# A gated convolution's input product in quarters: seven products of quarters in place of eight

## The reference, cut to what matters

```python
def shortconv(z, w):
    zp = jnp.pad(z, ((0, 0), (1, 1), (0, 0)))
    return w[0] * zp[:, :-2] + w[1] * zp[:, 1:-1] + w[2] * zp[:, 2:]

def odd_mixer(h, w_in, conv_w, w_out):
    bg, cg, u = jnp.split(h @ w_in, 3, axis=-1)
    return (bg * shortconv(cg * u, conv_w)) @ w_out
```

## Time and profile before

| what | value |
|---|---|
| median of three runs | 2458.86 us (2455.47 to 2461.43) |
| span of the profiled execution, first to last instruction | 2454.7 us |
| TensorE busy | 2323.3 us (95%) |
| VectorE busy | 855.8 us (35%) |
| input product of the gated convolution | 1705.74 to 1872.10 us of the span |

### The profile page before, as it was taken

The page is one execution under the profiler, slowest core; times in us unless marked ns, Lnnn a source line. Parts: engine busy times, 40 slices in busy tenths (PEclk is TensorE's granted clock), DMA queues, the critical chain, the costliest instruction groups (busy, mean ns, idle before and its releaser), DMA issues.

```text
span 2454.7 us, 22347 instructions
## 1 busy us (share of the span) xinstructions
PE 2323.3 (95%) x8986; PEld 1089.8 (44%) x8986; DVE 855.8 (35%) x1230; ACT 367.1 (15%) x697; POOL 65.3 (3%) x70
## 2 busy tenths in 40 slices
PE   7999899999999999879799999998999799999997
PEld 3443344444444455555544444443444454444443
DVE  3882354467006650782302222113111312222223
ACT  3224200001004110461210000002000110000000
POOL 1000000000010000000000000000000100000000
PEclk9999999999999999999899999999999799999999
DMA  9227234668300102000499999998010479999995
GB/s 356 111 73 274 86 137 157 234 236 328 142 0 26 43 35 69 35 1 1 206 412 421 429 428 428 429 427 307 11 57 1 205 312 429 429 428 429 429 428 229
DMA packets 105646, 565.62 MB, mean 230 GB/s; under 512 B 8424, under 2 KB 17006, under 8 KB 77934
## 3 DMA queue, kind: packets, MB, share of 16 engines
q1 hardware_dynamic: 104880, 563.55, 56.7%
q10 hardware_dynamic: 702, 1.18, 0.1%
HBM read 562.61 MB, written 2.10 MB: 230 GB/s over the span
## 4 chain that ended last, share of the span: by engine, by line
PE 83%; DMA 10%; DVE 5%; ACT 1%; issue 1%; SPq 0%; DVEq 0%; ACTq 0%
PE psum L973 38%; PE psum L1425 19%; DMA ring<-in_moe_w_gate_dram 7%; PE psum L1484 5%; PE psum L1440 5%; PE psum L1242 3%; PE psum L1353 2%; PE psum L1115 1%; DMA ring<-in_moe_w_down_dram 1%; DMA ring<-in_conv_w_pw_dram 1%; PE psum L1317 1%; PE psum L993 1%; DVE small L1766 1%; PE psum L1290 1%; PE psum L1033 1%
## 5 line engine op out<-in xcount | busy, mean ns | idle before, releaser
L1425 PE MATMUL psum<-ring,arena 128*64 128x512 f32 x3072 | 671.5, 595 | 20.3 <-DMA ring<-in_moe_w_gate_dram 13.0
L973 PE MATMUL psum<-hT,ring 128*128 128x512 f32 x1504 | 657.8, 598 | 15.0 <-ACT hT L665 12.0
L973 PEld LDWEIGHTS psum<-hT,ring 128*128 128x128 f32 x1504 | 287.4, 192 | 378.1 <-issue 366.1
L1425 PEld LDWEIGHTS psum<-ring,arena 128*64 128x64 f32 x3072 | 228.4, 137 | 449.0 <-issue 446.9
L973 PE MATMUL psum<-arena,ring 128*128 128x512 f32 x640 | 278.1, 593 | 0.0
L973 PEld LDWEIGHTS psum<-arena,ring 128*128 128x128 f32 x640 | 120.5, 190 | 149.7 <-issue 149.5
L1906 DVE TENSOR_TENSOR hT<-hT,psum 128x512 f32<-128x512 f32 x128 | 88.0, 687 | 244.1 <-PE psum L1484 244.1
L1440 PE MATMUL psum<-arena 128*128 128x128 f32 x1024 | 124.3, 281 | 4.0 <-DVE arena L1915 4.0
L1440 PEld LDWEIGHTS psum<-arena 128*128 128x128 f32 x1024 | 120.1, 197 | 15.5 <-issue 15.5
L1484 PE MATMUL psum<-arena 128*128 128x512 f32 x256 | 123.2, 619 | 0.0
L1578 DVE SCALAR_TENSOR_TENSOR xT<-psum,modv,xT 128x512 f32<-128x512 f32 x32 | 24.0, 751 | 246.0 <-PE psum L973 202.8
(11 more groups left out here) (216 smaller groups left out, 1636.2 us busy)
## 6 DMA issues: line engine op xcount, KB each, us to landing
ring<-in_moe_w_gate_dram SPq DMA_DIRECT2D x64, 2048.0 KB, 14.8
ring<-in_moe_w_up_dram SPq DMA_DIRECT2D x64, 2048.0 KB, 16.4
ring<-in_moe_w_down_dram SPq DMA_DIRECT2D x64, 2048.0 KB, 16.8
ring<-in_ada_w_dram SPq DMA_DIRECT2D x24, 2048.0 KB, 12.9
ring<-in_mlp_w_dram SPq DMA_DIRECT2D x16, 2048.0 KB, 11.4
ring<-in_w_mod_dram SPq DMA_DIRECT2D x12, 2048.0 KB, 12.8
ring<-in_conv_w_in_dram SPq DMA_DIRECT2D x6, 2048.0 KB, 18.7
ring<-in_attn_w_in_dram SPq DMA_DIRECT2D x5, 2048.0 KB, 8.0
```

The lines of the kernel that those rows point to most:

```text
L973: ins = pe.matmul(bank[:, 0:width], w[:, k, col:col + P], src(k), start=start and k == 0, stop=stop and k == kts - 1)
L1425: ins = pe.matmul(psum[64 * e:64 * e + 64, bank + nh, :], src[:, 4 * h + k, 64 * e:64 * e + 64], w[:, k, nh * N:(nh + 1) * N], start=h == ...
```

## The change

Each block of 1024x512 weights (a "unit", six of them in `UNITS`) is cut into four quarters of 512 rows by 256 columns, and `hT` into four quarters of 512 features by 256 tokens. The four quarters of the result come from seven products of quarters rather than eight, with the sums of Strassen's scheme in Winograd's form. Each product is 8 matmuls of 128x128 weights by 256 tokens: four for each half of a PSUM bank.

- VectorE forms three new sums of weights in SBUF and one in place for each unit (`w_sums`), and once four sums of the activations (`h_sums`), one of them in place.
- TensorE makes the products in a hand-written order in four banks for each unit; in three of them a second product is added onto the first.
- ScalarE copies the first product (M1) to SBUF, as TensorE then adds onto the same bank; for part 1 it also copies one finished quarter.
- VectorE adds the products up (`unit_out`) and multiplies each part into the one before it; `shortconv` runs the taps over four pieces at once in the program's order.
- The slots are released at the end of each unit. The memset of `hT` on GpSimd waits for the last tile of the last unit, and the output product waits for `mixed` by halves of four pieces.

```diff
-    for half in range(2):
-        for j in range(4 * half, 4 * half + 4):
-            T_O[j] = tiles(["act", "dve", "dve"])
...
+    for part, half in UNITS:
+        T_U.append(tiles(["dve", "act" if part == 1 else "dve", "dve", "dve"]))
+        add(blk(A["conv_w_in_2"][0], 0, part * D + half * N), ("tile_done", T_U[-1] + 4))
...
+            for u, (part, half) in enumerate(UNITS):
+                t = T_U[u]
+                act.wait_ge(S["part_done"], 3 * u + 1)
+                if u:
+                    act.wait_ge(*emptied(T_U[u - 1])(0))
+                act.activation(m1_sb, bank_pair(t + 1), ACT.Copy).then_inc(S["m1_copied"], 1)
+                if part == 1:
+                    act.wait_ge(S["tile_done"], t + 2)
...
+            def product(t, w, src, first=False):
+
+                for i in range(2):
+                    for k in range(4):
+                        ins = pe.matmul(psum[:, t % 6, H * i:H * i + H], w[:, k, P * i:P * i + P], src[:, k, :],
+                                        start=first and i == 0 and k == 0, stop=True, skip_group_check=True)
+                return ins
+
+            for u in range(len(UNITS)):
+                t = T_U[u]
+                slot = stream[oo + u][1]
+                arrived(pe, oo + u)
+                begin(t + 1)
+                if u == 0:
+                    pe.wait_ge(S["h_ready"], 8 * BIASED[MIX1] + 4)
+                product(t + 1, w_quarter(slot, 0, 0), hT[:, 0:4, 0:H], True).then_inc(S["part_done"], 1)
+                begin(t + 3)
+                if u == 0:
+                    pe.wait_ge(S["hsum_ready"], 1)
+                pe.wait_ge(S["wsum_ready"], 4 * u + 1)
+                product(t + 3, wsum[3 * u % 4], hsum1, True).then_inc(S["part_done"], 1)
+                begin(t)
+                if u == 0:
+                    pe.wait_ge(S["hsum_ready"], 2)
+                pe.wait_ge(S["wsum_ready"], 4 * u + 3)
+                product(t, wsum[(3 * u + 1) % 4], hsum2, True).then_inc(S["tile_done"], 1)
+                begin(t + 2)
+                if u == 0:
+                    pe.wait_ge(S["hsum_ready"], 4)
+                product(t + 2, w_quarter(slot, 0, 1), hsum3, True).then_inc(S["part_done"], 1)
+                pe.wait_ge(S["m1_copied"], u + 1)
+                product(t + 1, w_quarter(slot, 1, 0), hT[:, 4:8, 0:H]).then_inc(S["tile_done"], 1)
+                pe.wait_ge(S["part_read"], 2 * u + 1)
+                product(t + 2, w_quarter(slot, 1, 1), hsum4).then_inc(S["tile_done"], 1)
+                pe.wait_ge(S["wsum_ready"], 4 * u + 4)
+                pe.wait_ge(S["part_read"], 2 * u + 2)
+                product(t + 3, wsum[(3 * u + 2) % 4], hT[:, 4:8, H:N]).then_inc(S["tile_done"], 1)
...
+            def w_sums(u):
+
+                slot = stream[FIRST + u][1]
+                arrived(dve, FIRST + u)
+                s1, s2, s4 = (wsum[(3 * u + m) % 4] for m in range(3))
+                a11, a12, a21, a22 = (w_quarter(slot, r, c) for r, c in ((0, 0), (1, 0), (0, 1), (1, 1)))
+                dve.tensor_tensor(s1, a21, a22, ALU.add).then_inc(S["wsum_ready"], 1)
+                dve.tensor_tensor(a21, a11, a21, ALU.subtract).then_inc(S["wsum_ready"], 1)
+                dve.wait_ge(S["wsum_ready"], 4 * u + 1)
+                dve.tensor_tensor(s2, s1, a11, ALU.subtract).then_inc(S["wsum_ready"], 1)
+                dve.wait_ge(S["wsum_ready"], 4 * u + 3)
+                dve.tensor_tensor(s4, a12, s2, ALU.subtract).then_inc(S["wsum_ready"], 1)
+
+            def h_sums():
+
+                b11, b21 = hT[:, 0:4, 0:H], hT[:, 4:8, 0:H]
+                b12, b22 = hT[:, 0:4, H:N], hT[:, 4:8, H:N]
+                dve.wait_ge(S["h_ready"], 8 * BIASED[MIX1] + 4)
+                dve.tensor_tensor(hsum1, b12, b11, ALU.subtract).then_inc(S["hsum_ready"], 1)
...
+            def unit_out(u):
...
+                dve.wait_ge(S["tile_done"], t + 1)
+                dve.wait_ge(S["m1_copied"], u + 1)
+                dve.tensor_tensor(u2_sb, m1_sb, bank_pair(t), ALU.add).then_inc(FREE["dve"], 1)
+                dve.wait_ge(FREE["dve"], tile_free[t][1])
+                dve.wait_ge(S["part_done"], 3 * u + 3)
+                dve.tensor_tensor(u3_sb, u2_sb, bank_pair(t + 2), ALU.add).then_inc(S["part_read"], 1)
+                dve.wait_ge(S["part_read"], 2 * u + 1)
+                z22 = z[:, 2:4, H:N]
+                dve.tensor_tensor(z22 if part == 1 else u3_sb, u3_sb, bank_pair(t + 3), ALU.add)\
+                    .then_inc(S["part_read"], 1)
+                dve.wait_ge(S["part_read"], 2 * u + 2)
+                if part != 1:
+                    link(fold(z22, u3_sb))
+                if u + 1 < len(UNITS):
+                    w_sums(u + 1)
...
+            link(dve.memset(zpad[:, :, 0:1], 0.0))
+            link(dve.memset(zpad[:, :, N + 1:N + 2], 0.0))
+            w_sums(0)
             scale(MIX1, xT, hT, gain[:, 5, :])
...
+            h_sums()
+            for u in range(len(UNITS)):
+                unit_out(u)
```

More of the change, by code:

```diff
@@ L201, in block_kernel @@
     assert FIRST % RING == 0
-    T_O = {}
-    order_o = []
+    T_U = []
+    UNITS = [(part, half) for half in range(2) for part in (1, 2, 0)]
     T_H, T_AFF, T_POS = {}, {}, {}
@@ L359, in block_kernel @@
         prob1 = carve(arena, 8192, NK)
[L361 to L364, removed]
+        zpad = carve(arena, 0, 4, N + 2)
+        mixed = carve(arena, 4 * (N + 2), DT, N)
+        m1_sb, u2_sb, u3_sb = (carve(arena, 6152 + N * m, 2, H) for m in range(3))
+        wsum = [carve(arena, 8192 + 1024 * m, 4, H) for m in range(4)]
+        hsum1, hsum2 = (x[:, :, :].rearrange("p a b -> p (a b)").rearrange("p (k n) -> p k n", k=4) for x in (sq, tmp))
+        hsum4 = carve(K, KCOL["cos"][0], 4, H)
+        hsum3 = hT[:, 0:4, H:N]
         h_tok = carve(arena, 0, NT, D)
@@ L615, in _ @@
                 sum_squares(ROUTED[layer])
-                pool.wait_ge(S["tile_done"], T_WO + 8 if layer == 0 else T_O[DT - 1] + 3)
+                pool.wait_ge(S["tile_done"], T_WO + 8 if layer == 0 else T_U[-1] + 4)
                 pool.memset(hT[:, :, :], 0.0).then_inc(S["acc_zero"], 1)
@@ L947, in _ @@
             shift(MIX1, hT, modv[:, 3, 0:8])
[L948 to L953, removed]
+            for u, (part, half) in enumerate(UNITS):
[6 more added lines that the diff above has]
+                    act.wait_ge(S["tile_done"], t + 2)
+                    if half:
+                        act.wait_ge(S["conv3_done"], 1)
+                    act.activation(zpad[:, 0:2, 1:1 + H], bank_pair(t + 1), ACT.Copy).then_inc(FREE["act"], 1)
             squares(FFN1, xT, emptied(T_OO))
@@ L1518, in mixed_at @@
             def mixed_at(k):
[L1520 to L1529, removed]
+                return S["mixed_ready"], k // 4 + 1
@@ L1941, in _ @@
             experts(0)
-            scale(MIX1, xT, hT, gain[:, 5, :])
[L1943 to L1960, removed]
+            def w_sums(u):
[9 more added lines that the diff above has]
+                dve.tensor_tensor(s4, a12, s2, ALU.subtract).then_inc(S["wsum_ready"], 1)
@@ new lines, in shortconv @@
+            def shortconv(half):
+                for i in range(4):
+                    acc = mixed[:, 4 * half + i, :]
+                    for k in range(3):
+                        at = COL["w_conv3"] + 8 * k + 4 * half + i
+                        w, z = vecT[:, at:at + 1], zpad[:, i, k:k + N]
+                        if k == 0:
+                            link(dve.tensor_scalar(acc, z, w, None, ALU.mult))
+                        else:
+                            link(dve.scalar_tensor_tensor(out=acc, in0=z, scalar=w, in1=acc, op0=ALU.mult, op1=ALU.add))
@@ new lines, in unit_out, with fold @@
+            def unit_out(u):
+                part, half = UNITS[u]
+                t = T_U[u]
+                z = zpad[:, :, 1:N + 1] if part else mixed[:, 4 * half:4 * half + 4, :]
+                def fold(quarter, value):
+                    return dve.tensor_tensor(quarter, quarter, value, ALU.mult)
+                dve.wait_ge(S["tile_done"], t + 1)
[13 more added lines that the diff above has]
+                    w_sums(u + 1)
+                z11, z21, z12 = z[:, 0:2, 0:H], z[:, 2:4, 0:H], z[:, 0:2, H:N]
+                if part != 1:
+                    dve.wait_ge(S["tile_done"], t + 2)
+                    fold(z11, bank_pair(t + 1)).then_inc(FREE["dve"], 1)
+                dve.wait_ge(S["tile_done"], t + 3)
+                dve.tensor_tensor(z21 if part == 1 else u3_sb, u2_sb, bank_pair(t + 2), ALU.add).then_inc(FREE["dve"], 1)
+                if part != 1:
+                    dve.wait_ge(FREE["dve"], tile_free[t + 2][1])
+                    link(fold(z21, u3_sb))
+                dve.wait_ge(S["tile_done"], t + 4)
+                dve.tensor_tensor(z12 if part == 1 else u2_sb, u2_sb, bank_pair(t + 3), ALU.add).then_inc(FREE["dve"], 1)
+                dve.wait_ge(FREE["dve"], tile_free[t + 3][1])
+                if part != 1:
```

(11 more changed lines are left out.)

12 lines of the change are left out of this document (added).

## The result

The changed kernel takes 2440.56 us (median of four runs, 2437.28 to 2443.25) against 2457.16 us of the kernel before (four runs). The medians differ by 16.6 us, or 0.7%, where 2441.1 us was forecast. The ratio on record is 0.9927, 95% interval 0.9915 to 0.9939, so 15 to 21 us faster. The profiled execution has a span of 2437.2 us, against 2454.7 before.

What follows compares the result with a forecast made beforehand. TensorE, busy 95% of the span, was taken as the bound. Passes 145.0, later start 2.0 and clock 1.6 make 148.6 us against 166.36, a gain of 17.8, so 2441.1 us; range 2437 to 2446, with run scatter 2436 to 2449.

Steps and rivals of the forecast that it cites:

- The passes: TensorE's input product: 672 passes of 256 columns at 0.2158 us take 145.0 us; bounds 0.2145 and 0.220 a pass.
- The later start: The first product waits for four shifted pieces of hT, not one, so TensorE starts 2.0 us later.
- The clock at the start: The stage's first passes run at TensorE's lower clock, which costs 1.6 us, with ends of 0.8 and 3.0.
- Weight sums ahead of the reciprocal: VectorE's four sums at 1.22 us end 0.9 us before the root, so cost nothing; up to 2.6 us if not hidden.
- The sum between update and output product: The input-product stage takes 148.6 us against 166.36, a gain of 17.8 us.
- From span to median: The median of the runs stands 4.2 us above the profiled span, so 2436.9 becomes 2441.1 us.
- VectorE's timetable: In each 24.2 us unit VectorE delays TensorE nowhere; tightest is the read for product 6, with 2.7 us of room.
- The end: The output product's first four matmuls take 3.4 us and hide the second half of mixed, ready after about 1.6 us.
- Strided price: Rival: VectorE's additions cost the strided 2.13 us, only the stage's start pays, gain 15.2, 2443.7 us; chance 0.06.
- Heads of products: Rival: waits at 41 product starts cost TensorE time; at 0.83 us each, 34.0 us; chances 0.06, 0.04, 0.03 by rising price.
- Loads out of cover: Rival: TensorE's weight loads are not hidden behind 256-column passes, 17 us slower, 2476 us; chance 0.01.

Runs made afterwards that it cites:

- e1: Changed kernel with the third of the seven products of each unit made twice, so eight again; 2457.86 us, ratio 0.9997 to the kernel before.
- e2: Kernel before, each matmul of the input product split into two of 256 columns, no sums; 2459.10 us, ratio 1.0002.
- e10: Changed kernel, first product waiting for pieces of hT one by one, padding memsets moved behind the sums of hT, run again; 2436.95 us, ratio 0.9908.
- e3: Changed kernel with two more 1024-element additions on VectorE in each unit, ahead of the read product 6 waits for; 2439.90 us, ratio 0.9927.
- e4: Changed kernel with four more 1024-element additions on VectorE in each unit, ahead of the read product 6 waits for; 2458.05 us, ratio 0.9996.
- e8: Changed kernel with six more 1024-element additions on VectorE in each unit, ahead of the read product 6 waits for; 2480.50 us, ratio 1.0089.
- e9: Changed kernel as it is, measured again beside the version with an earlier first product; 2438.10 us, ratio 0.9912 to the kernel before.
- e7: Kernel before, each matmul of the input product split into four of 128 columns; 2466.96 us, ratio 1.0037.

## Why the prediction was right

- **The passes.** 672 x 0.2158 was the term that carries the forecast; the trace has 0.2158. That the eighth product is the gain is shown by e1 (21.0 us in the stage), that the shorter passes cost only 0.9 us by e2. The upper end of the range, 0.220 a pass, had no row behind it.
- **The later start.** 2.0 us predicted; the first pass comes 2.79 us after the first shift begins, against 0.87 before: 1.9. e10 starts 1.9 us earlier, and 1.3 of it are left at the end.
- **The clock at the start.** 1.6 us predicted, 1.9 lost in the first product (5.33 against 3.45). In other profiles it is 2.2 (e1, e3), 2.8 (e10) and 3.1 (e2), so the upper end of 3.0 was about right and the value taken on the low side.
- **Weight sums ahead of the reciprocal.** Additions of 1024 elements take 1.22 to 1.23 us, as taken from the slope, not 2.13. But in this profile the room of 0.9 us wasn't there: they ended 0.4 us after the root and held the reciprocal back by 0.17. The step that failed is the root's time, which I took as fixed. It isn't: the 16 passes of the norm took 9.18 us before and 7.67 after, at a granted clock of 0.81 and of 1.00, so the root came 1.5 us sooner after the update of `xT`. The norm's row before, and the windows of the norm before and after:

```profile
1690.51 9.18 PE L993 MATMUL psum<-sq,K 128*128 128x512 f32 x16 [2.32 <-ACT sq L652]
```

```profile
1690.50:1699.70 9.20, 9.18 (x16) 3.09 (x16) 3.84 (x6) 5.48 (x8) 0.00 (x0) 0.81 1.05 387
1692.80:1700.50 7.70, 7.67 (x16) 2.43 (x16) 7.49 (x12) 5.49 (x8) 0.00 (x0) 1.00 1.05 386
```

Where the norm took 9.18 us in a profile with the sums ahead of the reciprocal (e3, e4, e8, e9), they were hidden as predicted, and VectorE stood idle for 1.22 us before the reciprocal. In e9:

```profile
1699.31 3.35 DVE L1606 RECIPROCAL rstd<-rms 128x512 f32<-128x512 f32 x1 [1.22 <-ACT rms L666]
```

- **The sum between update and output product.** 17.8 predicted, less 0.3 (clock), less 0.2 (reciprocal), plus 1.5 (norm) gives 18.8, and 18.85 were measured. The 1.5 is luck and not the change, since the norm took 7.67 us too in the profiles of e2 and e7, whose kernels have neither the sums nor the products of quarters. The forecast of the span (2436.9, measured 2437.2) is better than its terms: the rest of the program happened to take back 1.35 us.
- **From span to median.** The 4.2 us were no fixed step. In every run on record the time stands 1.7 to 2.5 us above its own span; the rest of the 4.2 was a profiled execution faster than the median. The changed kernel's median stands 3.4 us above the span of its profile.
- **The range.** A gain of 13.6 to 19.5 us is 2439.4 to 2445.3 us; the 2437 to 2446 written down is a little wider than its terms. The measured 2440.56 lies in both.
- **VectorE's timetable.** Taps predicted to end 34.5 us after their unit's start; they ended at 1768.92, 34.2 after 1734.68. The read for product 6 left 2.5 us of room. e3 and e4 show that it is so: with more work on VectorE ahead of this read, TensorE stands still there and only there. The start of the stage was as tight once: the first sum of `hT` ended at 1711.52 and product 2 started at 1713.96, 2.4 us later (2.1 predicted).
- **The end.** The second half of `mixed` is done at 1857.23 and wanted 3.4 us after 1855.55. No gap.
- **Rivals.** Strided price: out by the rows. The price was also misread: L1887 reads its operands in order and writes its result with a stride (`quarters`), so it said nothing of additions that read quarters. Heads of products: the 41 later products start without a gap where their waits are met. Loads out of cover: out by e2, and e7 has loads each 0.111 us.

## What to carry to other kernels

The matmuls of a product on a TensorE that is never idle can be cut by an eighth, at the price of additions on an engine that is two thirds idle. It holds as long as the shorter matmuls still cover their weight loads, and each sum is ready before its product: make a timetable with the room at every wait, since the tightest one (here 2.5 us of a 24.2 us unit) is where it fails. Effects of 1 to 3 us in a 2440 us program are to be read in the rows between two fixed events, not in medians or spans.

## What the runs showed of the hardware that was not expected

- The granted clock can fall in or right behind gaps of 2.44 us: two of six such gaps were followed by about 3 us at 1.2 GHz, and all six of 4.95 us. Beside the gap itself, a stall of TensorE cost next to nothing or some 1.7 us at the short gap, and 1.5 to 3.2 us at the long one.
- The same 16 passes of the norm took 7.67 us in some profiles and 9.18 in others, of the same code, at a granted clock of 1.00 and 0.81. It moves a stage that hangs on them by 1.5 us from execution to execution.
- Weight loads of 128x128 float32 follow each other each 0.111 us, though each has a record of 0.19 us.
